# The last output chunk of a decoder trunk computed by token halves, with the final norm's sums taken token by token on the partitions

## What is computed

```python
def rmsnorm(x, g):
    xf = x.astype(jnp.float32)
    return xf * lax.rsqrt(jnp.mean(xf * xf, axis=-1, keepdims=True) + EPS) * g.astype(jnp.float32)
...
    y_prompt = rmsnorm(xp, norm_final_g).astype(x_prompt.dtype)
    y_sample = rmsnorm(xs, norm_final_g).astype(x_sample.dtype)
```

## Time and profile before

| what | value |
|---|---|
| median of 3 runs | 992.03 us (989.98 to 994.89) |
| profiled execution | 991.91 us |
| its span, first to last instruction | 990.2 us |
| mean granted TensorE clock | 0.985 |
| busy share: PE, PEld, DVE, ACT, POOL | 95%, 93%, 55%, 44%, 20% |

### The profile page before, as it was taken

One profiled execution on the slowest core, in us unless ns is written; L12 is line 12 of the kernel. 1 busy time (PEld: TensorE's weight loads), 2 busy tenths in 40 slices (PEclk: granted clock), 3 DMA queues, 4 the chain that ended last, 5 costly groups with the idle time before them and its releaser, 6 DMA issues.

```text
span 990.2 us, 21427 instructions
## 1 busy us (share of the span) xinstructions
PE 944.5 (95%) x8904; PEld 920.2 (93%) x8904; DVE 544.9 (55%) x929; ACT 431.4 (44%) x698; POOL 196.9 (20%) x377
## 2 busy tenths in 40 slices
PE   5899999999999997899999999999999999999994
PEld 4798899999999897899999999999999999999993
DVE  6998893793694483754333665444444444423334
ACT  5438527827746956422323344324332432222221
POOL 2598875732723021000000000000000000000000
PEclk9999999999999997999999999999999999999997
DMA  7422236263343343353242322232223223233212
GB/s 277 162 93 100 66 118 236 97 240 98 108 166 145 108 139 116 95 204 107 86 127 89 106 85 86 87 103 87 85 85 106 85 88 103 85 107 103 88 42 86
DMA packets 26987, 113.72 MB, mean 115 GB/s; under 512 B 3332, under 2 KB 3380, under 8 KB 25000
## 3 DMA queue, kind: packets, MB, share of 16 engines
q1 hardware_dynamic: 21744, 79.21, 25.6%
q0 software_dynamic: 2800, 24.65, 6.6%
q10 hardware_dynamic: 2376, 8.90, 2.3%
HBM read 99.35 MB, written 13.39 MB: 114 GB/s over the span
## 4 chain that ended last, share of the span: by engine, by line
PE 80%; DVE 7%; POOL 6%; ACT 4%; issue 2%; DMA 1%; DVEq 0%; ACTq 0%; POOLq 0%
PE G L1486 67%; PE G L1564 4%; PE Q L1486 2%; DVE c_samples L1258 1%; POOL pool_tmp L735 1%; PE Q L1581 1%; PE Q L1622 1%; PE Q L1609 1%; PE G L1662 1%; POOL s_setup L735 1%; POOL u_by_step L881 1%; ACT b_abar_by_step L422 1%; DVE x_scaled L1085 1%; ACT w_high L422 1%; PE G L1653 1%
## 5 line engine op out<-in xcount | busy, mean ns | idle before, releaser
L422 ACT ACTIVATE w_high<-raw 128x1024 fp32r<-128x1024 f32 (+1 forms) x147 | 154.9, 1056 | 303.8 <-PE G L1486 272.4
L987 DVE TENSOR_TENSOR w_low<-raw,w_high 128x1024 fp32r<-128x1024 f32 x146 | 180.2, 1235 | 179.8 <-ACT w_high L422 179.3
L1486 PE MATMUL G<-h_high,w_high 128*128 128x256 f32 x1344 | 273.9, 285 | 1.7 <-DVE x_residual L1413 0.9
L1486 PE MATMUL G<-h_low,w_high 128*128 128x256 f32 x1344 | 271.5, 283 | 0.0
L1486 PE MATMUL G<-h_high,w_low 128*128 128x256 f32 x1344 | 271.4, 283 | 0.0
L1486 PEld LDWEIGHTS G<-h_high,w_high 128*128 128x128 f32 x1344 | 209.4, 189 | 4.0 <-issue 1.6
L1486 PEld LDWEIGHTS G<-h_low,w_high 128*128 128x128 f32 x1344 | 209.3, 189 | 0.0
L1486 PEld LDWEIGHTS G<-h_high,w_low 128*128 128x128 f32 x1344 | 209.0, 189 | 0.0
L1486 PE MATMUL G<-hidden_low,w_high 128*128 128x256 f32 x352 | 70.9, 283 | 0.0
L1486 PE MATMUL G<-hidden_high,w_high 128*128 128x256 f32 x352 | 70.9, 283 | 0.0
L1486 PE MATMUL G<-hidden_high,w_low 128*128 128x256 f32 x352 | 70.6, 281 | 0.0
(11 more groups left out here) (381 smaller groups left out, 1538.7 us busy)
## 6 DMA issues: line engine op xcount, KB each, us to landing
raw<-wst SPq DMA_DIRECT2D x147, 512.0 KB, 3.5
c_samples<-c POOLq DMA_DIRECT2D x4, 2048.0 KB, 8.9
out_cs<-c_samples POOLq DMA_DIRECT2D x4, 2048.0 KB, 7.8
v_spread<-v_scratch ACTq DMA_DIRECT2D x4, 1024.0 KB, 5.6
x_tokens<-xt SPq DMA_DIRECT2D x4, 520.0 KB, 5.8
x_residual<-xt POOLq DMA_DIRECT2D x1, 2080.0 KB, 9.8
out_y<-x_residual ACTq DMA_DIRECT2D x8, 260.0 KB, 2.2
small<-small ACTq DMA_DIRECT2D x1, 1785.0 KB, 8.6
```

The costliest lines, as they stand in the source:

```text
L422: return act.activation(out, in_, ACT.Copy, **kw)
L987: tt(WL[n.slot()][:], raw[n.slot()][:], WH[n.slot()][:].bitcast(F32), ALU.subtract).then_inc(w_lo, 1)
L1486: last = mm(o, w[slot][:, c], h[:, k, c0_:c0_ + width], start=start and x == 0 and t == 0, stop=stop and x == n - 1 and t == 2)
```

## The change

The first seven chunks stay as they are. The eighth, and the norm behind it, are rewritten:

- PE runs the eighth chunk's 66 products of the first 256 tokens, then its 66 products of the last 264 (L1856 of the new kernel). Only the first pass waits for weights. In the code, chunks 6 and 7 now stand behind the loop, which runs two times instead of three.
- For each half, DVE adds the products to `X1` and squares the half itself (into `fsq[1]`); ACT no longer squares the eighth chunk, and the eighth chunk's squares aren't added to `facc`.
- The sums of squares are made with the data as the stationary operand and one column of ones as the moving one (`sum_squares`): a tile of 128 tokens gives one column of PSUM with its tokens on the partitions. There are two tiles in the first half and three in the second, the last of which is the last 128 tokens (it overlaps the one before it). Each tile has one product for `facc` and one for the eighth chunk's squares.
- ACT takes the root of 2 or 3 columns, DVE their reciprocal, and PE spreads them back over all partitions (`spread_inverse`): a column, broadcast to 128 columns, is the stationary operand and an identity matrix the moving one. The identity is built by POOL in the space of `YS`, right behind the load of `X1`.
- DVE scales the eight chunks of one half with the factor read from PSUM. SP stores the eight pieces of the first half (128 x 256 each); the second half's pieces (128 x 264) are stored by SP for even m and by ACT for odd m.
- The first half's small products stand in the second half's stream: its sums behind 12 of the 66 products, its spreading behind 24.
- ACT issues a root of a constant ahead of the tail, so that the table load stands there.

```diff
@@ scalar
             for m, n in steps(act, KC, 3, 2, N_DOWN, loops=3):
                 for j in range(3):
-                    if m.i is not None or m.static < KC - 1:
+                    if m.i is not None or m.static < LAST:
                         after(n.plus(j))
+                if m.i is None and m.static == LAST:
+                    continue
...
-            act.wait_ge(fsq_summed, 2)
-            act.activation(fr[:, 0:256], Q[:, 2, 0:256], ACT.Sqrt, bias=eps[:, 0:1], scale=1.0 / D)
-            act.activation(fr[:, 256:T], Q[:, 3, 0:264], ACT.Sqrt, bias=eps[:, 0:1], scale=1.0 / D).then_inc(fin_root, 1)
-            for m in range(KC):
-                act.wait_ge(y_ready, m + 1)
-                act.dma_start(y_o[:, m, :], X1[:, m, :]).then_inc(y_out, 16)
-            act.wait_ge(y_out, 16 * KC)
+            act.activation(junk_a[:], eps[:], ACT.Sqrt)
+            for half, (c0_, w) in enumerate(HALVES):
+                t0, n_t = TILES[half][0], len(TILES[half])
+                act.wait_ge(fin_summed, half + 1)
+                act.activation(rt[:, t0:t0 + n_t], Q[:, half, t0:t0 + n_t], ACT.Sqrt, bias=eps[:, 0:1], scale=1.0 / D).then_inc(fin_root, 1)
+            c0_, w = HALVES[1]
+            for m in range(1, KC, 2):
+                act.wait_ge(y_ready, KC + m + 1)
+                act.dma_start(y_o[:, m, c0_:c0_ + w], X1[:, m, c0_:c0_ + w]).then_inc(y_out, 16)
+            act.wait_ge(y_out, 16 * 2 * KC)
@@ sync
+            for half, (c0_, w) in enumerate(HALVES):
+                for m in range(0, KC, 1 + half):
+                    sp.wait_ge(y_ready, KC * half + m + 1)
+                    sp.dma_start(y_o[:, m, c0_:c0_ + w], X1[:, m, c0_:c0_ + w]).then_inc(y_out, 16)
@@ gpsimd
             pool.dma_start(X1[:], xt).then_inc(x1_in, 16)
+            pool.wait_ge(x1_in, 16)
+            own.do(pool.memset(ident_late[:], 1.0))
+            own.do(pool.affine_select(out=ident_late[:], in_=ident_late[:], compare_op=ALU.is_ge, fill=0.0, base=0,
+                                      pattern=[[1, P]], channel_multiplier=-1))
+            pool.affine_select(out=ident_late[:], in_=ident_late[:], compare_op=ALU.is_ge, fill=0.0, base=0,
+                               pattern=[[-1, P]], channel_multiplier=1).then_inc(late_ident, 1)
@@ vector
-            dve.wait_ge(fin_root, 1)
-            dve.reciprocal(fr[:], fr[:]).then_inc(fr_ready, 1)
-            dve.wait_ge(fr_ready, 2)
-            for m in range(KC):
-                stt(X1[:, m, :], X1[:, m, :], g_fin[:, m:m + 1], fr[:], ALU.mult, ALU.mult).then_inc(y_ready, 1)
+            for half, (c0_, w) in enumerate(HALVES):
+                t0, n_t = TILES[half][0], len(TILES[half])
+                dve.wait_ge(last_half, half + 1)
+                own.do(tt(X1[:, LAST, c0_:c0_ + w], X1[:, LAST, c0_:c0_ + w], G[:, B + half, 0:w], ALU.add))
+                tt(fsq[1][:, c0_:c0_ + w], X1[:, LAST, c0_:c0_ + w], X1[:, LAST, c0_:c0_ + w], ALU.mult).then_inc(last_squared, 1)
+                dve.wait_ge(fin_root, half + 1)
+                dve.reciprocal(rt[:, t0:t0 + n_t], rt[:, t0:t0 + n_t]).then_inc(fin_inverse, 1)
+                dve.wait_ge(fin_spread, half + 1)
+                for m in range(KC):
+                    stt(X1[:, m, c0_:c0_ + w], X1[:, m, c0_:c0_ + w], g_fin[:, m:m + 1], Q[:, 2 + half, 0:w],
+                        ALU.mult, ALU.mult).then_inc(y_ready, 1)
@@ tensor
-            for m, n in steps(pe, KC, 3, 2, N_DOWN, loops=3, peel=2):
+            for m, n in steps(pe, KC, 3, 2, N_DOWN, loops=2, peel=2):
+                if m.i is None and m.static == LAST:
+                    continue
...
-            pe.wait_ge(x2_added, KC + 1)
-            mm(Q[:, 2, 0:256], ones[:], facc[:, 0:256], start=True, stop=True)
-            mm(Q[:, 3, 0:264], ones[:], facc[:, 256:T], start=True, stop=True).then_inc(fsq_summed, 1)
+            def sum_squares(half):
+
+                for src, value, s in ((facc, x2_added, KC), (fsq[1], last_squared, 1 + half)):
+                    pe.wait_ge(value, s)
+                    for i in TILES[half]:
+                        last = mm(Q[:, half, i:i + 1], src[:, tokens_in(i)], ones[:, 0:1],
+                                  start=src is facc and i == TILES[half][0], stop=src is not facc, skip_group_check=True)
+                last.then_inc(fin_summed, 1)
+
+            def spread_inverse(half):
+                pe.wait_ge(late_ident, 1)
+                pe.wait_ge(fin_inverse, half + 1)
+                for i in TILES[half]:
+                    part = ident_late[:] if i < SC else ident_late[:, P - NS:P]
+                    at = P * (i - TILES[half][0])
+                    last = mm(Q[:, 2 + half, at:at + part.shape[1]], rt[:, i:i + 1].broadcast_to([P, P]), part, start=True, stop=True)
+                last.then_inc(fin_spread, 1)
+
+            n = At(N_DOWN + 3 * LAST)
+            pe.wait_ge(x2_ready, KC)
+            for half, (c0_, w) in enumerate(HALVES):
+                for j in range(3):
+                    if half == 0:
+                        pe.wait_ge(w_lo, n.plus(j).val(1, 1))
+                    cols = range(DOWN_CUT[j], DOWN_CUT[j + 1])
+                    for x, k in enumerate(cols):
+                        for t, (wt, h) in enumerate(((WH, HIDH), (WH, HIDL), (WL, HIDH))):
+                            last = mm(G[:, B + half, 0:w], wt[n.plus(j).slot()][:, P * x:P * x + P], h[:, k, c0_:c0_ + w],
+                                      start=j == 0 and x == 0 and t == 0, stop=j == 2 and k == F_TILES - 1 and t == 2)
+                        if half == 1 and j == 0 and x == 3:
+                            sum_squares(0)
+                    if half == 1 and j == 0:
+                        spread_inverse(0)
+                last.then_inc(last_half, 1)
+            sum_squares(1)
+            spread_inverse(1)
```

## The result

| | before | after |
|---|---|---|
| median | 989.16 us (987.42 to 994.89, 15 runs) | 984.95 us (981.59 to 989.76, 15 runs) |
| profiled execution | 991.91 us, span 990.2 | 989.16 us, span 987.4 |

The ratio is 0.9948, with a 95% interval of 0.9930 to 0.9967: 0.52% faster, where 0.56% was forecast (986.5 of 992.03). The medians themselves lie 4.2 us apart, 0.43%, inside that interval. The change did nearly what the sum said.

What follows compares the result with a forecast made beforehand. PE was taken to bound the kernel up to the eighth chunk's last product, a serial tail following. The tail shrinks by 6.8 us, PE's stream grows by 1.4: 5.4 less than 991.91 gives 986.5, range 984.8 to 989.4.

Steps and rivals of the forecast that it cites:

- The bound: Whole kernel: PE bounds it up to the eighth chunk's last product, then a serial tail of 15.99 us.
- Order of the products: Eighth chunk: 132 products stay 132, 15.8 us; the third unit of weights is ready with slack 3.0, price 0.
- cover of the first half's chain: Eighth chunk: first half's sums, factor and scaling lie beside the second half's products, slack 1.6, price 0.
- Small products in the stream: PE's second-half stream: the first half's sums 0.81 us and spreading 0.60 us add 1.4 us together.
- The new tail: From the last product to the end: handoffs, arithmetic, scaling and last store sum to 9.18 us instead of 15.99.
- The clock in the tail: Rival: low clock behind the last product lengthens sums and spreading by some 0.65 each, 987.8; chance 0.18.
- Stores: End of kernel: a 1056-byte row costs 0.044 to 0.064 us, 0.35 to 0.51 per store; last landing 2.37.
- The estimate worked out from that page's figure: Second half's stores: 138 GB/s would mean 0.98 us per store, 7.8 us in place of 3.4, time 991.
- The step that failed: Final sum: 5.4 us off the profiled execution's 991.91, taken as 0.1 from the median 992.03, gives 986.5.
- the range's lower end: Range of the time: best ends of the bounds give 985.9, medians can be off by one, so 984.8.
- two rivals about the end of the kernel: Low clock in the tail, 987.8, chance 0.18; clock falling inside the eighth chunk's second half, 995.7, chance 0.04.
- Chances: Whole kernel, with the line at half a percent, 987.1: faster 0.57, same 0.40, slower 0.03.

Runs made afterwards that it cites:

- first_half_behind: Changed kernel with the first half's sums and spreading moved behind the last big product; 991.15 us, ratio 1.0004 to the kernel before.
- warm: Changed kernel with unread products in PE's idle pieces of the tail; 986.68 us, ratio 0.9965 to the kernel before.
- filled_middle: Changed kernel with unread products in PE's three idle pieces of the middle; 980.68 us, ratio 0.9908 to the kernel before.
- whole_stores: Changed kernel without separate first-half stores, each chunk stored whole behind its second half's scaling; 987.93 us, ratio 0.9983 to the kernel before.
- halves_only: Changed kernel keeping the halves, with the old all-ones sums and wide reciprocal, no spreading; 985.50 us, ratio 0.9956 to the kernel before.
- mixed: Changed kernel with the first half's factor by the all-ones matrix, the second's by columns and spreading; 986.75 us, ratio 0.9965 to the kernel before.

## Why the prediction was right and where it was wrong

**The bound.** Right: PE without a pause up to the last product, and a serial tail of 16 us behind it.

**Order of the products, cover of the first half's chain.** Right. PE's chain shows no idle piece in the second half; the first half's scaling ended 1.9 us ahead of the last product, 1.6 were forecast. `first_half_behind` shows what the cover is worth: 15.3 - 9.4 - 1.4 = 4.5 us, of which 0.6 is the low clock under its second sums.

**Small products in the stream.** Forecast 1.4, measured 1.4 by the length of the whole chunk (17.20 against 15.82). That it fits so well is luck: the four records of the spreading took 0.44, or 0.11 each instead of 0.15, and what they saved went into the longer steps of the big products behind the two groups, which the sum didn't have.

**The new tail.** The sum of 9.18 against 9.4. Addition and square 0.44 each (0.43, 0.42), sums 0.84 (0.86), root 0.28 (0.30), reciprocal 0.19 (0.18), scaling 3.29 (3.36), handoffs 0.3 (0.28). Two terms were off, in opposite directions: the spreading took 1.43 instead of 0.98, for it ran at the low clock, and the last store took 987.4 - 981.92 - 3.29 = 2.2 instead of 2.37. At the full clock the spreading's term was too high (0.78 and 0.82 in `warm` and `filled_middle`), so the sum came close by a miss that a second one partly made good.

**The clock in the tail.** The forecast gave it 0.18 as a rival worth 1.3 us. It came, but later than the rival had it: the sums still ran at the full clock, and only the spreading paid, 0.6 (1.43 against 0.82 in `filled_middle` and 0.78 in `warm`). The sign named for it was there, a granted clock of 0.50 from 980.1 on, ahead of the spreading at 980.46.

**Stores.** Right that a row of 1056 bytes costs near its bytes: 0.050, between the bounds of 0.044 and 0.064. The page that spoke against small stores, the Trainium skill's "DMA: Bandwidth & Descriptors", section Bandwidth, gives 138 GB/s for transfers of 64 KB, measured on loads from HBM. Here eight stores of 132 KB (1.08 MB in all) kept DVE's pace of 0.41 each, over 320 GB/s. The estimate worked out from that page's figure, 991, was wrong for stores that follow one another on two queues. In one thing the trace agrees with the page: a larger transfer is cheaper for its bytes, 0.088 us for a row of 2080 bytes against 0.050 for one of 1056, some 10%. What cost 2.4 us in `whole_stores` is not the size of the transfers but that all 2.13 MB leave in the tail instead of 1.08.

**What the forecast didn't ask** is which part carries the gain. Its sum credits the reciprocal with 3.41 - 0.18. That is right as a difference between two sums, but the halves alone already bring the tail's reciprocal to 1.81 (`halves_only`), and the spreading took the rest.

**The step that failed** is the one from the profiled execution to the median: "that execution lies 0.1 from the median of the runs, 992.03, so the forecast is 986.5", and with it the range's lower end, for which medians were allowed to be "off by one". The runs showed in its place a base of 989.16 in 15 runs, 2.9 lower, and a kernel whose executions reach from 987.00 to 995.75, with medians of whole sets between 989.16 and 993.54; a median of three can be off by more than one. The trace had the reason in it: the clock's rows were read for two rivals about the end of the kernel, and not for what they say of the level. A low clock behind three idle pieces, of a length that varies from one execution to the next, goes with most of the scatter: 6.8 us lie between the executions at 0.987 and those at 0.980, more than the whole change. A forecast of a ratio, 0.9944, would have stood inside the measured interval.

**Chances.** Measured 0.52% faster, almost on the line of half a percent, and the chances, 0.57 and 0.40, left open on which side it would fall.

## What to carry to other kernels

Where a serial tail stands behind a stream of products, split the last step of the stream so that half of the tail, its stores included, runs beside the rest; this alone was worth all of the gain here, and a cleverer form of an operation that is then half as wide added nothing as long as its own products ran at the low clock. Read a granted clock below 1.00 behind idle pieces of PE as a cost in its own right: here unread products in three pieces of 2 to 4 us gave some 6 us and took most of the scatter away. To price small products put into a stream, measure the whole stream with and without them, not their own rows. Compare versions by the part of the chain that they change, and forecast a ratio when three runs differ by as much as the change.

## What the runs showed of the hardware that I had not expected

Filling PE's idle time of about 9.5 us with products whose results are thrown away made the kernel before faster by 0.6% (0.9937) and the changed one by 4 to 7 us (980.68 against 984.95 and 987.77 in other sets, and 6 us against `mixed` and `warm` in its own). The same 2.2 us piece was followed by a low clock in some executions (0.57 from 419.70 on in the change) and by the full one in others (1.00 from 418.80 on in the kernel before); what decides it stays open. A float32 product with one moving column costs two records of 0.10 us in a stream, and one with 128 moving columns two of 0.11; behind such a group the first big product holds PE for 0.20 us instead of 0.12. At the granted clock of 0.50 the same six records of the spreading took 1.43 us, against 0.78 and 0.82 at 1.00.
